# Where the tiles that the matmuls read start within the SBUF partition: a two-block, fp32-accurate network on one core

## The reference

```python
for i in range(2):
    h = layer_norm(DN_ALPHA * h + 0.5 * swiglu(h, ffn_w_in[i, 0], ffn_w_out[i, 0]), ln_g[i, 0], ln_b[i, 0])
    m = gla_mixer(h, ...) if i == 0 else retention_mixer(h, ...)
    h = layer_norm(DN_ALPHA * h + m, ln_g[i, 1], ln_b[i, 1])
    h = layer_norm(DN_ALPHA * h + 0.5 * swiglu(h, ffn_w_in[i, 1], ffn_w_out[i, 1]), ln_g[i, 2], ln_b[i, 2])
# second block
merged = jnp.sum(up * g, axis=2)          # three attention branches, gated
x = _layer_norm(DEEPNORM_ALPHA * x + merged @ w_out, ln1_g, ln1_b)
h = jnp.square(jax.nn.relu(x @ w_ff1))
x = _layer_norm(DEEPNORM_ALPHA * x + h @ w_ff2, ln2_g, ln2_b)
```

## The kernel before

| tile | start | past a multiple of 512 |
|---|---|---|
| weights_raw, weights_hi, weights_lo | 16512, 41088, 65664 | 128 |
| operand_hi, operand_lo | 90240, 98432 | 128 |
| normalised, residual, ln_rows, constants, squares | 106624 to 133248 | 128 |
| row_sum to minus_half (nine small tiles, 480 bytes) | 137344 | 128 and on |
| first tile of each phase (silu_gate, gla_qT, ret_qkT, att_qT) | 137824 | 96 |
| hidden_hi, hidden_lo | 143968, 156256 | 96 |
| gla_w_low_hi, gla_w_low_lo | 212576, 216672 | 96 |
| ret_out_lo, ret_out_hi | 195168, 211552 | 96 |
| att_p, att_pT, att_w_small_hi, att_w_small_lo, att_out_hi | 176928 to 209696 | 288 |

## Time and profile before

### The profile page before, as it was taken

How to read it: one execution, slowest core, us unless ns; L and a number is a source line. 1 busy time by engine, 2 the same in 40 slices (tenths; PEclk the granted TensorE clock), 3 DMA queues, 4 the chain that set the end, 5 groups by cost and what they waited for, 6 DMA issues and landing times.

```text
span 1594.3 us, 23577 instructions
## 1 busy us (share of the span) xinstructions
PE 1569.8 (98%) x9892; PEld 1392.9 (87%) x9892; DVE 897.1 (56%) x855; ACT 699.2 (44%) x617; POOL 126.3 (8%) x149
## 2 busy tenths in 40 slices
PE   8999999999999999999999999999999999999998
PEld 7999888789998999989878799998999788889887
DVE  5444565564445544466457654447585456674555
ACT  5343355344334433443334444334536556353442
POOL 1000011110001000013121100001003200010000
PEclk9999999999999999999999999999999999999999
DMA  7555554355554655555444465556444334455551
GB/s 297 185 185 185 185 196 174 106 185 185 185 184 158 215 191 184 179 201 218 165 166 154 167 223 185 179 190 212 160 162 161 106 133 184 159 186 190 188 184 71
DMA packets 41727, 283.94 MB, mean 178 GB/s; under 512 B 4912, under 2 KB 5232, under 8 KB 8752
## 3 DMA queue, kind: packets, MB, share of 16 engines
q1 hardware_dynamic: 37728, 270.55, 47.2%
q0 software_dynamic: 2368, 8.59, 1.6%
q10 hardware_dynamic: 1552, 3.64, 0.7%
HBM read 281.65 MB, written 1.05 MB: 177 GB/s over the span
## 4 chain that ended last, share of the span: by engine, by line
PE 93%; DVE 3%; ACT 2%; POOL 2%; issue 1%; DMA 0%; DVEq 0%; POOLq 0%; ACTq 0%
PE psum L1363 29%; PE psum L1367 29%; PE psum L1366 29%; PE psum L1375 1%; ACT squares L427 1%; PE psum L1637 1%; DVE normalised L866 1%; POOL att_p L379 1%; POOL ln_rstd L290 0%; DVE normalised L835 0%; DVE weights_lo L805 0%; PE psum L1726 0%; PE psum L1780 0%; POOL ln_rstd L289 0%; PE psum L1748 0%
## 5 line engine op out<-in xcount | busy, mean ns | idle before, releaser
L805 DVE TENSOR_TENSOR weights_lo<-weights_raw,weights_hi 128x2048 fp32r<-128x2048 f32 x249 | 573.8, 2306 | 468.4 <-ACT weights_hi L406 466.2
L406 ACT ACTIVATE weights_hi<-weights_raw 128x2048 fp32r<-128x2048 f32 (+1 forms) x256 | 485.0, 1895 | 446.2 <-PE psum L1367 437.4
L1363 PE MATMUL psum<-operand_hi,weights_hi 128*128 128x256 f32 x1952 | 553.9, 284 | 0.0
L1366 PE MATMUL psum<-operand_lo,weights_hi 128*128 128x256 f32 x1952 | 552.1, 283 | 0.0
L1367 PE MATMUL psum<-operand_hi,weights_lo 128*128 128x256 f32 x1952 | 552.1, 283 | 0.0
L1363 PEld LDWEIGHTS psum<-operand_hi,weights_hi 128*128 128x128 f32 x1952 | 374.1, 192 | 4.6 <-issue 2.2
L1366 PEld LDWEIGHTS psum<-operand_lo,weights_hi 128*128 128x128 f32 x1952 | 374.2, 192 | 2.1
L1367 PEld LDWEIGHTS psum<-operand_hi,weights_lo 128*128 128x128 f32 x1952 | 374.2, 192 | 0.0
L1363 PE MATMUL psum<-weights_hi,operand_hi 128*128 128x512 f32 x512 | 205.3, 401 | 6.5 <-DVE weights_lo L848 4.7
L1366 PE MATMUL psum<-weights_lo,operand_hi 128*128 128x512 f32 x512 | 201.0, 393 | 0.0
L1363 PE MATMUL psum<-weights_hi,hidden_hi 128*128 128x512 f32 x480 | 190.2, 396 | 0.0
(11 more groups left out here) (248 smaller groups left out, 1084.5 us busy)
## 6 DMA issues: line engine op xcount, KB each, us to landing
weights_raw<-in_weights SPq DMA_DIRECT2D x256, 1024.0 KB, 4.8
ln_rows<-in_ln_rows POOLq DMA_DIRECT2D x16, 512.0 KB, 4.8
normalised<-in_x SPq DMA_DIRECT2D x2, 512.0 KB, 6.1
ret_constants<-in_ret_constants ACTq DMA_DIRECT2D x1, 1024.0 KB, 5.9
out<-normalised SPq DMA_DIRECT2D x4, 256.0 KB, 2.0
att_constants<-in_att_constants ACTq DMA_DIRECT2D x1, 576.0 KB, 4.5
gla_w_low<-in_gla_w_low ACTq DMA_DIRECT2D x1, 512.0 KB, 3.5
att_w_small<-in_att_w_small ACTq DMA_DIRECT2D x1, 512.0 KB, 3.9
```

Source lines behind the costliest of these rows:

```text
L406: nc.scalar.activation(w_hi[:, s, whole], raw[:, s, whole], ACT.Copy).then_inc(hi_split, 1)
L805: nc.vector.tensor_tensor(w_lo[:, s, :], raw[:, s, :], w_hi[:, s, :].bitcast(F32), ALU.subtract).then_inc(lo_split, 1)
L1363: mm(out, a_hi, b_hi, start=start, stop=False, skip_group_check=True)
L1366: mm(out, a_hi, b_lo, start=False, stop=False, skip_group_check=True)
```

## The change

The order of allocations changes, and nothing else. The nine small LayerNorm tiles and two small tiles of the GLA phase come first, then a tile of 216 float32 that nothing reads or writes, then the large ones. `weights_raw` moves behind `weights_lo`. In the GLA phase `gla_low` moves behind the three tiles of the low-rank weight; in the attention phase the large tiles move ahead of the small ones.

```diff
+ROW_START = 216
...
-        raw = sb("weights_raw", [P, RING, TILE])
-        w_hi = sb("weights_hi", [P, RING, TILE], F32R)
-        w_lo = sb("weights_lo", [P, RING, TILE], F32R)
-        x_hi = sb("operand_hi", [P, KC, TOK], F32R)
...
         row_sum = sb("row_sum", [P, 2 * TB])
...
         minus_half = sb("minus_half", [P, 8])
+        g_bg = sb("gla_b_gate", [P, GLA_HEADS])
+        g_ss = sb("gla_sumsq", [P, 8])
+        sb("to_a_row", [P, ROW_START])
+        w_hi = sb("weights_hi", [P, RING, TILE], F32R)
+        w_lo = sb("weights_lo", [P, RING, TILE], F32R)
+        raw = sb("weights_raw", [P, RING, TILE])
+        x_hi = sb("operand_hi", [P, KC, TOK], F32R)
+        x_lo = sb("operand_lo", [P, KC, TOK], F32R)
+        xn = sb("normalised", [P, TB, D])
...
-            g_low = sb("gla_low", [GLA_RANK, TOK], F32, ph)
             g_tail = sb("gla_w_low", [P, KC, P], F32, ph)
             g_tail_hi = sb("gla_w_low_hi", [P, KC, P], F32R, ph)
             g_tail_lo = sb("gla_w_low_lo", [P, KC, P], F32R, ph)
+            g_low = sb("gla_low", [GLA_RANK, TOK], F32, ph)
...
             a_v = sb("att_v", [P, 3, TB, HEADS * HEAD_DIM], F32, ph)
+            a_p = sb("att_p", [P, HEADS, CAUSAL], F32, ph)
+            a_pt = sb("att_pT", [P, HEADS, CAUSAL], F32, ph)
+            with ExitStack() as sub:
+                a_tail = sb("att_w_small", [P, KC, P], F32, sub)
+                a_tail_hi = sb("att_w_small_hi", [P, KC, P], F32R, sub)
+                a_tail_lo = sb("att_w_small_lo", [P, KC, P], F32R, sub)
+                a_qi = sb("att_qiT", [P, 8, TOK], F32, sub)
+            a_oh = sb("att_out_hi", [P, 12, TOK], F32R, ph)
+            a_ol = sb("att_out_lo", [P, 12, TOK], F32R, ph)
             a_ki = sb("att_kiT", [P, TOK], F32, ph)
             a_wf = sb("att_wi_fg", [P, TB, IDX_HEADS + HEADS], F32, ph)
             a_lf = sb("att_log_f", [P, 3, TB, HEADS], F32, ph)
             a_cT = sb("att_minus_cT", [HEADS, TOK], F32, ph)
...
```

More of the change, by code:

```diff
@@ L89, in build @@
         minus_half = sb("minus_half", [P, 8])
+        g_bg = sb("gla_b_gate", [P, GLA_HEADS])
[7 more added lines that the diff above has]
+        xn = sb("normalised", [P, TB, D])
+        resid = sb("residual", [P, TB, D])
+        ln_rows = sb("ln_rows", [P, 2, D])
+        cst = sb("constants", [P, 4, P])
+        ident, tri, later_of, ones = (cst[:, i, :] for i in range(4))
+        squares = sb("squares", [P, D])
         bank = ctx.enter_context(nc.psum_tensor("psum", [P, 8, NCOL], F32))
@@ L119, in build @@
             g_tail_lo = sb("gla_w_low_lo", [P, KC, P], F32R, ph)
+            g_low = sb("gla_low", [GLA_RANK, TOK], F32, ph)
             g_wg = sb("gla_w_gate", [GLA_RANK, GLA_HEADS * GLA_DK], F32, ph)
-            g_bg = sb("gla_b_gate", [P, GLA_HEADS], F32, ph)
             g_gain = sb("gla_gain", [P, GLA_DV], F32, ph)
             g_cst = sb("gla_constants", [P, TOK + GLA_HEADS * P], F32, ph)
-            g_ss = sb("gla_sumsq", [P, 8], F32, ph)
             g_junk = sb("gla_junk", [P, GLA_DV], F32, ph)
@@ L156, in build @@
             a_sum = sb("att_sum", [P, TB, HEADS], F32, ph)
-            a_p = sb("att_p", [P, HEADS, CAUSAL], F32, ph)
-            a_pt = sb("att_pT", [P, HEADS, CAUSAL], F32, ph)
             causal, negdist, strict = (a_cst[:, i, :] for i in range(3))
[L160 to L166, removed]
             relu = a_pt[:, :, :].rearrange("p h c -> p (h c)")[:, 0:2048].rearrange("p (b c) -> p b c", b=2)
```

## The result

The changed kernel takes 1587.55 us (median, 1587.38 to 1588.97) against 1598.01 us for the kernel before; the ratio is 0.9939, 95% interval 0.9925 to 0.9953. It is faster by 0.6%. The executions of each kernel lie in two groups about 1.6 us apart (before 1596.24 beside 1597.84 to 1598.25, after 1587.38 to 1587.63 beside 1588.97), and the two medians fall into different ones, so that group against group the gain is 8.8 to 9.2 us where the medians differ by 10.5. The forecast was 1531 us in a range of 1495 to 1604: the sign was right, the gain of 67 us over six times too large. R1, at 1589 us, is what happened.

A forecast was written before the change was run, and what follows sets the result against it. The prediction took TensorE's matmul spacing to bound the kernel. Gains of 35.1 (256 columns), 10.5 (512 on operand) and 21.2 us (512 on phase tiles) summed to 67, so 1598.2 - 67 = 1531 us, range 1495 to 1604.

The forecast's parts named there:

- R1: Rival: only the phase tiles gain, since weights against operand already have distance zero; 9.2 us, 1589 us, chance 0.22.
- What bounds the kernel: TensorE, busy 1569.8 of 1594.3 us with all feeders behind it, so only the spacing of its matmul starts matters.
- part (5): ScalarE, VectorE, GpSimd and DMAs at new addresses: they have cover, gone only below about 100 ns a matmul.
- Does it depend on addresses?: Three-pass matmuls in the trace: tile placement moves their spacing by 3 to 6 ns; no tile lies at +0.
- Part (1), 256 columns, 35.1 us: 5856 matmuls with 256 moving columns and weights stationary: spacing falls from 120.0 to 114 ns; bounds 0 and 49.8 us.
- Part (2), 10.5 us: 1504 matmuls with 512 columns and stationary operand: spacing falls from 228 to 221 ns; bounds 0 and 18.0 us.
- Part (3): 1712 matmuls with 512 columns on phase tiles: from 233.4 to 221 ns, 21.2 us; lower gain 9.2, at best 29.8.
- The loss itself: Three-pass matmuls lose 13 to 20 ns beyond their columns, laid to streams that need a word in every cycle.
- R4: Rival: slower, since coinciding reads cost; 256-column matmuls go to 123 ns, 17.6 us lost, 9.2 won, 1607 us, chance 0.13.
- R2: Rival: nothing changes, the loss belongs to full-rate streams and tile differences come from something else; 1598 us, chance 0.10.
- The chances: Forecast 0.45, R1 0.22, R2 0.10, R4 0.13; faster in all 0.77, within about 0.2% 0.10, slower 0.13.

The follow-up runs named there:

- e8_both: The changed kernel with the operand tiles 448 bytes and the hidden tiles 192 bytes past a multiple of 512; 1558.59 us, ratio 0.9761 to the kernel before.
- e2_all_plus32: The changed kernel with its filler 32 bytes longer, so every tile behind it starts 32 bytes further; 1588.0 us, ratio 0.9944 to the kernel before.
- the sweeps: TensorE alone, not the network, with stationary and moving tiles at many offsets; at distance 0, 120.0 ns with 256 columns and 226.7 with 512.
- e1_phase_only: The kernel before with one more unused tile of 32 bytes, which moves only the phase tiles; 1588.25 us, ratio 0.9943 to the kernel before.
- e7_steps: TensorE alone, the FFN step's order of matmuls at set distances; 256-column stretch at distance 64: 117.8 ns behind hidden at 0, 113.6 at 192.
- e4_x192: The changed kernel with a smaller front filler and the operand tiles 192 bytes past a multiple of 512; 1570.2 us, ratio 0.9833 to the kernel before.
- e5_x448: The changed kernel with a smaller front filler and the operand tiles 448 bytes past a multiple of 512; 1569.63 us, ratio 0.9833 to the kernel before.

## Why the prediction was wrong

*What bounds the kernel*, and that only the spacing of starts matters: right, and the balance above. Each microsecond of spacing came back as a microsecond of span, in the change and in e8_both, and part (5), the cover of the feeders, held down to 113.4 ns.

*Does it depend on addresses?* Yes, but I left open which property of the address, and then priced the change as if the absolute one might be worth something. The rows could not tell the two apart, since the moving tile of every three-pass product started at +128, so that distance and the stationary tile's own start sort the pairs alike; e2_all_plus32 and the sweeps decided it. The rows did show that weights and operand both started at +128, a distance of 0, and the diff leaves that distance at 0. R1 says this and gets 1589.

*Part (1), 256 columns, 35.1 us*: the step that failed. It took a start on a multiple of 512 bytes to bring the spacing from 120.0 down to 114 ns. 120.0 stayed 120.0 and the gain was 0 us, because the distance between the two tiles stayed 0. The 114 was the middle between a bound from another form (line 1553) and `gla_w_low` at 117.0; but that row's stationary tile lay 32 bytes off the moving one's place, and the change removed just such distances. It spoke against the gain: `gla_w_low` itself went up to 119.6. A spacing near 114 does exist, as e8_both shows, at a distance that the change doesn't make.

*Part (2), 10.5 us*: failed by the same step, 0.2 us.

*Part (3)*: its lower bound 9.2 us is what came, 7.4 on hidden and 1.5 on the others; the 21.2 in the sum was the mis-sized term, since its 221 rested on the same guess as part (2).

*The loss itself*, laid to streams that need a word in every cycle: nothing spoke against it. bfloat16 came at 109.2 and 215.8 ns, and fp32r at distance 0 loses 13.3 ns at 256, 384 and 512 columns alike. That it is the word in every cycle which costs is not shown.

*R4* was wrong in its second step of 3 ns, but its reading of the 256-column rows (coincidence costs 3 ns) is the part of the prediction that points to the faster version. *R2* and the granule of 16 bytes that the Trainium skill names in "SBUF — State Buffer", section "Specifications (TRN2)", don't account for the rows: e1_phase_only moves tiles from one multiple of 32 to another and gains 0.6%.

*The chances*: 0.22 on R1 against 0.45 on the forecast. Against R1 stood that the 256-column rows sort the other way round; that was no evidence against it, for R1 needs only that distance decides, not that zero is best at each width. Distance sorted every pair of tiles in the trace, as the stationary tile's own start did, and the row of 512 was not tested by any.

## What to carry to other kernels

When matmul starts are spaced wider than their columns, read the spacing by pair of tiles and set it against the distance between the starts of the stationary and the moving tile, before anything is aligned: unused tiles of 32 to 448 bytes in the right places were the whole edit here. All of this was run for fp32r; the one shift of bfloat16, by 96 bytes, changed nothing. A change that moves all tiles alike leaves all distances as they are, so ask of a rewrite which differences it alters, not which values. And a spacing can have two steady values at one placement, so price it in the order in which the kernel issues its products.

## What the runs showed of the hardware

- fp32r matmuls are spaced by 113.3 to 120.0 ns with 256 moving columns and 226.7 to 234.3 with 512, bfloat16 by 109.2 and 215.8 at either shift tried (0 and 96 bytes); the mean granted clock was 0.997 to 0.999 in all runs. Plain fp32 took 430 ns where its columns need 426.7, at one placement. At distance 0 fp32r loses 13.3 ns beyond its columns at 256, 384 and 512 alike.
- Within multiples of 32 bytes the fp32r spacing goes by the distance modulo 256, to about 1.5 ns between runs, beside the two values at 64. Best at 512 columns: 0 (226.7), then 192 (228.9). Best at 256 columns: 64, with 113.3 or 117.8; 224 gives a steady 116.7; 0 gives 120.0.
- At a distance of 64 two spacings are each stable over hundreds of matmuls. A hidden product ahead led to 113.3 when its distance was 192 (e7_steps, and 38 of 38 in e8_both) and to 117.8 when it was 0 (38 of 38 in e4_x192 and e5_x448). A product with stationary `operand` at 192 or 448 led to either, a transpose in the network mostly to 113.3, a plain fp32 matmul in e7_steps to 117.8.
- What the two reads contend for was not found. Narrower weight loads change the spacing without removing the loss, so a cost per column loaded cannot be all of it; that two streams meet in something with a period of 256 bytes is an argument from the table, not a thing shown.
